# Sixteen tokens moved from dense products to gathered rows in the last stage of a one-core block

## The reference

```
act = gelu(einsum('ted,td->te', expert_u[e], t)) * gates
out = einsum('te,ted->td', act, expert_v[e])
```

## Time and profile before

| | |
|---|---|
| profiled execution, its own time | 4046.6 us |
| its span | 4045.0 us |
| clock granted to TensorE, mean | 0.996 |
| TensorE busy | 3982.8 us, 98% |
| TensorE's weight loads busy | 3441.5 us, 85%; one takes 188 ns |
| VectorE busy | 2477.6 us, 61% |
| ScalarE busy | 1227.1 us, 30% |
| GpSimd busy | 928.9 us, 23% |
| row steps (L1881) | 127 of 2346 ns, waits ahead of them 29.9 us |
| one-element gathers (L636) | 128 of 1535 ns |
| chain that ended last | TensorE 63%, VectorE 7%, DMA 4%, issue 3% |

### The profile page before, as it was taken

One profiled execution on the slowest core, in us unless ns is written; L12 is line 12 of the kernel. 1 busy time (PEld: TensorE's weight loads), 2 busy tenths in 40 slices (PEclk: granted clock), 3 DMA queues, 4 the chain that ended last, 5 costly groups with the idle time before them and its releaser, 6 DMA issues.

```text
span 4045.0 us, 53754 instructions
## 1 busy us (share of the span) xinstructions
PE 3982.8 (98%) x19149; PEld 3441.5 (85%) x19149; DVE 2477.6 (61%) x3455; ACT 1227.1 (30%) x1299; POOL 928.9 (23%) x670
## 2 busy tenths in 40 slices
PE   8999999999999999999999999999999999999998
PEld 5887777787788788888888888888899999999997
DVE  8565777469534654535676663222257787887885
ACT  4333222344223322222333332222222222222222
POOL 1100000332111345453000000000023444444432
PEclk9999999999999999999999999999999999999999
DMA  4543333652543454546777778666768888888883
GB/s 175 194 141 132 118 118 123 208 183 100 190 144 142 155 181 158 180 158 211 241 239 241 239 245 309 219 214 218 229 233 309 302 324 301 326 305 323 300 322 131
DMA packets 240049, 867.73 MB, mean 215 GB/s; under 512 B 22600, under 2 KB 61016, under 8 KB 172272
## 3 DMA queue, kind: packets, MB, share of 16 engines
q1 hardware_dynamic: 96720, 454.07, 30.7%
q10 hardware_dynamic: 94080, 204.49, 16.3%
q0 software_dynamic: 49184, 208.36, 14.8%
HBM read 768.25 MB, written 232.81 MB: 247 GB/s over the span
## 4 chain that ended last, share of the span: by engine, by line
PE 63%; DVE 7%; DMA 4%; issue 3%; ACT 2%; POOL 0%; DVEq 0%; SPq 0%; ACTq 0%
PE mm L1959 15%; PE mm L1960 15%; PE mm L1961 15%; DMA raw<-stream 3%; PE pv L1959 2%; PE pv L1961 2%; PE pv L1960 2%; DVE wlo L1127 2%; PE sc L1961 1%; PE sc L1960 1%; PE sc L1959 1%; DVE acc L1881 1%; ACT whi L684 1%; PE st L1961 1%; PE st L1960 1%
## 5 line engine op out<-in xcount | busy, mean ns | idle before, releaser
L1127 DVE TENSOR_TENSOR wlo<-raw,whi 128x2048 fp32r<-128x2048 f32 x329 | 756.2, 2299 | 762.0 <-ACT whi L684 757.4
L684 ACT ACTIVATE whi<-raw 128x2048 fp32r<-128x2048 f32 x378 | 723.7, 1915 | 492.6 <-issue 209.0
L1959 PE MATMUL mm<-t_hi,whi 128*128 128x512 f32 x2048 | 799.2, 390 | 4.3 <-DVE t_lo L1688 3.1
L1960 PE MATMUL mm<-t_lo,whi 128*128 128x512 f32 x2048 | 797.5, 389 | 0.0
L1961 PE MATMUL mm<-t_hi,wlo 128*128 128x512 f32 x2048 | 797.0, 389 | 0.0
L1959 PEld LDWEIGHTS mm<-t_hi,whi 128*128 128x128 f32 x2048 | 384.7, 188 | 86.1 <-DVE t_lo L1688 6.4
L1961 PEld LDWEIGHTS mm<-t_hi,wlo 128*128 128x128 f32 x2048 | 384.5, 188 | 80.4
L1960 PEld LDWEIGHTS mm<-t_lo,whi 128*128 128x128 f32 x2048 | 384.7, 188 | 77.5
L1959 PE MATMUL mm<-hn_hi,whi 128*128 128x512 f32 x960 | 377.4, 393 | 4.8 <-DVE wlo L1127 4.8
L1960 PE MATMUL mm<-hn_lo,whi 128*128 128x512 f32 x960 | 374.3, 390 | 0.0
L1961 PE MATMUL mm<-hn_hi,wlo 128*128 128x512 f32 x960 | 373.9, 389 | 0.0
(11 more groups left out here) (438 smaller groups left out, 7228.8 us busy)
## 6 DMA issues: line engine op xcount, KB each, us to landing
raw<-stream SPq DMA_DIRECT2D x380, 1024.0 KB
ev_d<-stream ACTq DMA_DIRECT2D x128, 1024.0 KB, 6.2
up_d<-sgl ACTq DMA_DIRECT2D x128, 256.0 KB, 2.1
g_d<-gst ACTq DMA_DIRECT2D x12, 2048.0 KB, 11.6
gg<-g_d SPq DMA_DIRECT2D x15, 1536.0 KB
gl<-up_d SPq DMA_DIRECT2D x120, 192.0 KB
spill<-stage ACTq DMA_DIRECT2D x44, 256.0 KB, 2.0
xm_d<-xms POOLq DMA_DIRECT2D x12, 512.0 KB, 5.5
```

The costliest lines, as they stand in the source:

```text
L684: act.activation(whi[:, k, :], raw[:, k, :], ACT.Copy).then_inc(hi_done, 1)
L1127: dve.tensor_tensor(wlo[:, k, :], raw[:, k, :], whi[:, k, :].bitcast(F32), ALU.subtract)\
L1959: pe.matmul(out, lh, rh, start=start, stop=False)
L1960: pe.matmul(out, lh, rl, start=False, stop=False)
```

## The change

Of the 384 dense tokens the last 16 (`TP` = 368 to 384) leave the products. `down` now multiplies 368 columns, and `add_down` adds 368. Gates, high and low halves are still made for 384.

Those 16 tokens are gathered with eight partitions a token (`LANES` = 8): partition p serves token p mod 16 and every eighth part of its 128 slots, so 16 more row steps (`LS`), each again 128 rows of 8 KB, into an accumulator of their own (`lane_acc`). In the last group at v = 3 sixteen products of `lane_acc` with a 128 x 16 matrix of ones and zeros (`lane_of`) sum the eight partitions of each token; `add_lanes` adds the result to `h2`.

The slots of the 16 tokens are brought into that layout through DRAM (three stores and one load on ScalarE's queue ahead of the one-hot stage), and VectorE computes the indices between two splits of the up stage.

The row steps are now 144 (`STEPS`): the first 16 for the lanes, 128 as before. They begin in group 0 at v = 2. All groups of VectorE are written out. GpSimd issues 16 one-element gathers for the lanes ahead of the first, and the batches of nine stand ahead of row 10 + 9b. `weights` stands directly ahead of the step that uses it first.

The tiles `gl` are now two with places of their own; some small tiles are added; some waits in the last group count the new product and its add.

```diff
+LT = 16
+TP = TD - LT
+LANES = P // LT
+LS = SLOTS // LANES
+STEPS = LS + SLOTS
...
-            activations(0)
-            for s in range(3, SLOTS):
-                if s % BATCH == 3:
-                    pool.wait_ge(ac_done, s // BATCH + 1)
-                    activations(s // BATCH + 1)
-                rows(s)
+            for s in range(LS):
+                activation_of(lane_el, lane_e, s)
+            for n in range(3, STEPS):
+                if n >= LS - 6 and (n - LS + 6) % BATCH == 0 and n - LS + 6 < SLOTS:
+                    b = (n - LS + 6) // BATCH
+                    pool.wait_ge(ac_done, b + 1)
+                    activations(b)
+                rows(n)
...
+                    act.wait_ge(slot_done, 2 * PH)
+                    for v in range(3):
+                        act.dma_start(lanes_d[:, :, v, :].rearrange("l t s -> t l s"), slot[P - LT:P, v, TB - 2, :, :]
+                                      .rearrange("p h k -> p (h k)").rearrange("p (l s) -> p l s", l=LANES))\
+                            .then_inc(lanes_moved, 16)
+            act.wait_ge(lanes_moved, 48)
+            act.dma_start(lanes[:], lanes_d.rearrange("l t v s -> (l t) v s")).then_inc(lanes_moved, 16)
...
-                    dve.tensor_tensor(h2[:, 4 * q + b, 0:TD], h2[:, 4 * q + b, 0:TD], vo2[q % 2][b][:, 0:TD],
+                    dve.tensor_tensor(h2[:, 4 * q + b, 0:TP], h2[:, 4 * q + b, 0:TP], vo2[q % 2][b][:, 0:TP],
                                       ALU.add).then_inc(v_free, 1)
+            def weigh(n):
+
+                dve.wait_ge(gv_in[n % 3], 16 * (n // 3) + 16)
+                to, w, s = (lane_acc, lane_ac, n) if n < LS else (acc, ac, n - LS)
+                if s == 0:
+                    dve.tensor_scalar(to[:], gv[n % 3][:], w[:, 0:1], None, ALU.mult).then_inc(acc_done, 1)
                 else:
+                    dve.wait_ge(acc_done, n)
+                    dve.scalar_tensor_tensor(to[:], gv[n % 3][:], w[:, s:s + 1], to[:], ALU.mult, ALU.add)\
                         .then_inc(acc_done, 1)
+            def lane_weights():
+
+                dve.wait_ge(el_in, 16 * LS)
+                dve.tensor_tensor(lane_ac[:], lane_el[:], lanes[:, 0, :], ALU.mult).then_inc(ac_done, 1)
+                dve.wait_ge(ac_done, 1)
+
+            def weights(b):
+
+                s0, s1 = BATCH * b, min(BATCH * (b + 1), SLOTS)
+                dve.wait_ge(el_in, 16 * (LS + s1))
+                dve.tensor_tensor(ac[:, s0:s1], el[:, s0:s1], gate3[:, s0:s1], ALU.mult).then_inc(ac_done, 1)
+                dve.wait_ge(ac_done, b + 2)
+
+            def gathered(steps):
+                for n in steps:
+                    if n == 0:
+                        lane_weights()
+                    if n >= LS and (n - LS) % BATCH == 0:
+                        weights((n - LS) // BATCH)
+                    weigh(n)
+
+            def down_group(g, steps):
+
+                dve.wait_ge(gn_in, 16 * g + 16)
                 for v in range(8):
                     down_lo(g, v)
...
                     gate((g + 1) % 2, v, 8 * g + 8 + v)
                     act_low(g % 2, v, 8 * g + 8 + v)
                     if v % 2 == 1:
                         add_down(g, v // 2)
+                    gathered(steps[v])
...
-            down_group(0, False)
-            down_group(1, True, peeled=True)
-            with dve.Fori(2, GROUPS_D - 1) as g:
-                down_group(g, True)
+            down_group(0, share((0, 0, 1, 1, 1, 1, 1, 1)))
+            for g in range(1, GROUPS_D - 1):
+                down_group(g, share((2, 1, 1, 1, 1 if g % 3 == 0 else 2, 1, 1, 1)))
...
-                        last = mm3(vo2[q % 2][b][:, 0:TD], *w(k, 512 * jj + P * b), actb[:, (g + 1) % 2, 0, 4 * h + jj, :],
-                                   actb[:, (g + 1) % 2, 1, 4 * h + jj, :], h == 0 and jj == 0, h == 1 and jj == 3)
+                        last = mm3(vo2[q % 2][b][:, 0:TP], *w(k, 512 * jj + P * b),
+                                   actb[:, (g + 1) % 2, 0, 4 * h + jj, 0:TP],
+                                   actb[:, (g + 1) % 2, 1, 4 * h + jj, 0:TP], h == 0 and jj == 0, h == 1 and jj == 3)
...
+                if v == 3:
+
+                    pe.wait_ge(acct_free, 1)
+                    for d in range(KC):
+                        last = pe.matmul(vo2[0][0][:, LT * d:LT * d + LT], lane_acc[:, P * d:P * d + P], lane_of[:],
+                                         start=True, stop=True)
+                    last.then_inc(acct_done, 1)
```

More of the change, by code:

```diff
@@ L220, in build @@
         acc = S("acc", [P, D], F32, 96)
+        lane_acc = S("lane_acc", [P, D], F32, 192)
+        lane_t = S("lane_t", [P, P], F32, 196)
+        lane_p = S("lane_p", [P, 3], F32, 196.5)
+        lane_f = S("lane_f", [P, 3, LS], F32, 196.625)
+        lanes = S("lanes", [P, 3, LS], F32, 205.25)
+        lane_v = S("lane_v", [P, LS], U32, 205.625)
+        lane_e = S("lane_e", [P, LS], U32, 205.75)
+        lane_el = S("lane_el", [P, LS], F32, 205.875)
+        lane_ac = S("lane_ac", [P, LS], F32, 206)
+        lane_of = S("lane_of", [P, LT], F32, 206.125)
         gv = [S(f"gv{i}", [P, D], F32, kb) for i, kb in enumerate((140, 148, 184))]
@@ L646, in _, with rows @@
-            for s in range(3):
-                rows(s)
+                    activation_of(el, idx_e, s)
+            def rows(n):
+                if n >= 3:
+                    pool.wait_ge(acc_done, n - 2)
+                index = lane_v[:, n:n + 1] if n < LS else idx_v[:, 0, n - LS:n - LS + 1]
+                pool.indirect_dma_start(gv[n % 3][:], None, ev_d, bass.IndirectOffsetOnAxis(ap=index, axis=0))\
+                    .then_inc(gv_in[n % 3], 16)
+            for n in range(3):
+                rows(n)
@@ L659, in _ @@
+            pool.wait_ge(acct_done, 5)
             pool.memset(sq_sum[:], 0.0).then_inc(qsum_done, 1)
@@ L1897, in down_group @@
+            def down_group(g, steps):
+                dve.wait_ge(gn_in, 16 * g + 16)
                 for v in range(8):
                     down_lo(g, v)
-                    if v == 0 and not slots:
-                        dve.wait_ge(gn_in, 16 * g + 16)
                     dve.wait_ge(upn_in[v % 2], 64 * g + 16 * (v // 2) + 16)
@@ L1919, in _, with share @@
             dve.wait_ge(h2_copied, 32)
-            down_group(0, False)
-            down_group(1, True, peeled=True)
-            with dve.Fori(2, GROUPS_D - 1) as g:
-                down_group(g, True)
+            at = [0]
+            def share(counts):
+                out = []
+                for c in counts:
+                    out.append(range(at[0], at[0] + c))
+                    at[0] += c
+                return out
+            down_group(0, share((0, 0, 1, 1, 1, 1, 1, 1)))
+            for g in range(1, GROUPS_D - 1):
+                down_group(g, share((2, 1, 1, 1, 1 if g % 3 == 0 else 2, 1, 1, 1)))
             def add_gathered():
@@ L1929, in add_gathered, with add_lanes @@
                                       vo2[0][b][:].rearrange("p (d t) -> p d t", t=P), ALU.add).then_inc(acct_free, 1)
-            last = BATCH * (GROUPS_D - 2)
+            def add_lanes():
+                dve.wait_ge(acct_done, 5)
+                dve.tensor_tensor(h2[:, :, TP:TD], h2[:, :, TP:TD],
+                                  vo2[0][0][:, 0:KC * LT].rearrange("p (d t) -> p d t", t=LT), ALU.add)\
+                    .then_inc(acct_free, 1)
             for v in range(8):
@@ L1935, in _ @@
                 if v == 0:
-                    weights(last, SLOTS - last, SLOTS)
-                    dve.wait_ge(ac_done, GROUPS_D - 1)
-                    for s in range(last, SLOTS):
-                        weigh(s, s % 3, s // 3 + 1)
+                    gathered(range(at[0], STEPS))
                 if v == 2:
                     add_gathered()
+                if v == 3:
+                    add_lanes()
                 if v % 2 == 1:
```

83 lines of the change are left out of this document (41 added, 42 removed).

## The result

The changed kernel took 4114.65 us (median of 4 runs, 4112.96 to 4117.77) against 4052.01 for the kernel before: ratio 1.0158, 95% interval 1.0144 to 1.0172. That is 63 us slower, where 4078 was forecast, outside the range of 4014 to 4108. The profiled execution took 4115.6 us, 69 more than that of before. TensorE's mean granted clock fell from 0.996 to 0.986.

A forecast was written before the change was run, and what follows sets the result against it. TensorE was taken to bound the kernel before, VectorE the changed one. Groups 2 to 14 +22, group 0 +8.8, group 1 -1.5 and the last +0.5 gave +30 us, so 4078, range 4014 to 4108.

The forecast's parts named there:

- gather batches: Groups 2 to 14: weights formed directly ahead of their step leave VectorE waiting at fourth rows, 62 us where 27.8 stood.
- Products: Down stage, TensorE: 6144 products lose 16 columns, 6.67 ns each, 41.0 us in all where TensorE stays the bound.
- rival D: TensorE's weight load is the bound, so fewer columns give nothing; 4084 us, chance 0.02.
- VectorE's own work: Groups 2 to 14: 721.6 us busy plus 70.3 of fixed wait, 60.9 a group against 64.0 of TensorE.
- Load leg: Groups 2 to 14: VectorE's waits for the high half of the weights and TensorE, 39 us, bounds 17 and 47.
- Group 0: First down group: VectorE stands 15 us for sixteen one-element gathers, so group 1 starts 8.8 us later.
- Group 1: Second down group, already written out: one more step fits at TensorE's pace, 66.5 becomes 65, -1.5 us.
- Last group: End of the down stage: units save 2.6 us, sixteen small fp32 products cost 3; net +0.5.
- Set-up: Up stage: 15 small VectorE operations and four small DMAs on ScalarE's queue cost nothing; possible stall taken as 0.
- B: Rival: the gather batches cost no more than before, 28 us instead of 62; 4043 us, chance 0.16.
- C: Rival: TensorE stays the bound, all DMA waits fit into 3.1 us a group; 4015 us, chance 0.19.
- E: Rival: fetching VectorE's some ten times longer program beside busy DMAs costs time; 4100 us, chance 0.05.

The follow-up runs named there:

- b_late: The kernel before with each batch's weights formed directly ahead of the group's first row step instead of at the group's head; 4094.77 us, ratio 1.0111.
- b_unroll: The kernel before with VectorE's groups 2 to 14 written out and nothing else; 4066.33 us (seven runs), ratio 1.0052.
- s_lump: a_spread with four more full-width VectorE operations in one place (ahead of the step of v = 5) in groups 2 to 14; 4139.2 us, ratio 1.0217.
- s_thin: a_spread with one more half-width VectorE operation ahead of the first step of every v in groups 2 to 14; 4109.57 us, ratio 1.0143.
- a_gn: The changed kernel with VectorE's wait for the gates moved behind the first split of a group; 4115.91 us, ratio 1.0164.
- a_spread: The changed kernel without batches: each one-element gather is issued behind a row gather, nine steps ahead of its use; 4034.76 us, ratio 0.9967.
- b_spread: b_unroll with each one-element gather issued behind a row gather instead of in batches, no tokens moved; 4042.83 us, ratio 0.9979.

## Why the prediction was wrong

The direction and the mechanism were right, the size was half: groups 2 to 14 lost 55 us where +22 was forecast. The step that failed is the price of the gather batches, 62 us for 86.2 measured; beside it the sum had no term for TensorE's clock.

*Products and rival D.* Products are 166.7 ns apart (3738.28 and 3738.45 above), as forecast. Rival D, the weight load as bound, is out.

*VectorE's own work.* Forecast 721.6 busy and 70.3 of fixed wait; measured 723.6 and 71.7. Load leg: forecast 39; measured 28.3 + 12.0 + 1.8 = 42.1. These terms held.

*The gather batches: the step that failed.* "The fourth row comes 24.0 us after the first step's start", and "Together 62 us". The positions were right: all thirteen batches stall at their fourth row, the longest (10.05, 9.7, 8.1) among those with a double step inside. But the time from first step to fourth row was 23.7 to 28.8 us, 25.8 in the mean of the thirteen. That is 13 x 1.8 = 23.4 us. The waits at the fourth rows came to 80.9, 18.9 more than forecast, as VectorE itself was a little later there; three at fifth rows (steps 56, 65 and 128), which the sum did not have, add 5.3. The 86.2 are 24.2 above the forecast and above its bound of 80, and most of the 33 us that the stretch lies above its forecast of 893.

The batch itself was mis-sized. It took 18.1 us in the mean (16.9 to 19.4) against 16.8 before (twelve batches, 16.1 to 17.4), and I had carried over the length of the earlier trace rows, 16.6; that is 1.5 of the 1.8 us. The two fences of one stall show why it is not a constant. The first gather starts inside the row step of 3701.44, which ends at 3703.79, and ends at 3704.63, 0.84 later. The next starts inside the split that ends at 3705.99 and ends at 3706.83, again 0.84 later. The one of 3707.13, which starts beside no long operation, takes 0.95. In groups 2 to 14 of the changed kernel 66 gathers were longer than 1.2 us. Each of them started inside a row step (37) or a split (29) and ended 0.8 us behind that instruction; the 51 short ones started beside neither. Placing the batch directly at a row step does not lengthen it by itself: in b_late it stands there too, and all twelve batches of groups 2 to 14 took 16.03 us. In its loop VectorE begins the step 0.39 us behind the start of the forming of the weights, and the first gather begins 0.04 later (the two lines under b_late): it took 0.95. In the written-out changed kernel the step begins 0.20 behind and the first gather 0.24 later, well inside it; in eleven of thirteen batches it took 2.95. These 2.0 us are nearly the whole way from 16.0 to 18.1. Written out at the old place, in b_unroll, ten of twelve batches took 17.7 to 18.7 us, with 51.6 us of waits. So it is the written-out code, at either place, that goes with the longer batches.

The Trainium skill (SBUF — State Buffer, "Who interferes with whom") says that whoever issues first gets the shared ports for a whole instruction and the other blocks fully. The trace agrees for gathers behind VectorE; the other way round it shows nothing of the kind: the 16 splits that started inside a gather of 0.95 us took 2.29 us, like the others. The section also holds, as inferred, that a `tensor_tensor` takes only the read side and does not hold up descriptor writing. 29 gathers outlasted a split, which is one; but a gather also reads its indices (`idx_e`) from SBUF, so no run here tells which of its parts was held up. I had weighed this rule only as a reason for shorter batches, since a stalled VectorE blocks nothing. The stall begins when most of the batch is over.

*The clock: a term left out.* The sum held no price for what follows a gap. The slower pace (22.3 us in groups 2 to 14, 18.2 of it in ten stretches at half speed, and 4.1 in group 0; before, 1.8 in all of these together) is the other side of the loss, and s_lump against s_thin shows that it is real time. It may not be added to the 24.2 above: the two are accounts of the same stretch, by VectorE and by TensorE. Part of VectorE's 42.1 of load leg is waiting for a TensorE at half speed; how much was not separated.

*Group 0.* Forecast: next split at 2988.5, fifth unit near 2991, group 1 at 3023. Measured: 2988.45, 2990.86, and 3025.7. The last 2.7 us are half-speed products behind the gap of 5.85 us. A wait for the gates had moved ahead of the first split, which the prediction did not read from the diff (7.70 us of VectorE, a second gap of TensorE); a_gn shows that it costs nothing, being ahead of the longer one. *Group 1*: 68.4, forecast 65; it had one gap of 2.7 us and 1.7 of slower pace where none were expected. *Last group*: +1.0, forecast +0.5. Sixteen fp32 products of 16 columns took 3.64 us, forecast 3 within 1.5 to 8:

```profile
4046.38 3.64 PE L2431 MATMUL pv<-lane_of,lane_acc 128*128 128x16 f32 x32
```

*Set-up.* The down stage began at 2946 instead of 2945: nothing, as said.

*The rivals.* B (28 us of stalls) and C (stalls fit) did not come in this schedule; a_spread comes near to C's world and lands at 4034.8 (C said 4015). E, code fetch, had nothing to show: in groups 2 to 14 no waits of VectorE put down to issue, and b_spread written out at TensorE's exact pace.

## What to carry to other kernels

A batch of small gathers on the queue that also feeds the main loop is a blackout. Its price is its length and the landing of the next row (25.8 us here) less what the buffers hold. Issue small gathers one by one between the large ones; here that turned +63 us into -15, and 9 of the 15 come without the change under study. Price a batch at the place, and in the code, where it will run: count the long VectorE operations that its members start under. And when a sum makes TensorE wait in one piece of several microseconds, add the products at half speed behind each gap; the same waiting in eight small pieces had almost none. A gain of the engine that is 99% busy is worth only the slack of the next one: 41 us of columns gave 13, 26 and nothing that can be told in three schedules.

## What the runs showed of the hardware

- A one-element indirect gather takes 0.95 us, or until 0.83 us behind the end of a 128 x 2048 row step or split inside which it starts (up to 2.99). Those that began at its very start did not lengthen: twelve in b_late began 0.04 us behind it and took 0.95. In a_spread, where each starts behind a row gather, the mean of all 128 was 1.24 us, in the changed kernel 1.73. Adds of 128 x 368 from PSUM did not lengthen any of the 12 that started under one.
- Half speed behind gaps: in the changed kernel's groups 2 to 14 there were eleven gaps of 3.3 to 9.0 us. Ten were followed by 8 to 18 products 0.31 us apart, one (of 3.4 us) was not, and neither was any of the shorter ones, the longest 2.9 us. A stretch cost 1.1 to 2.5 us. That is no limit to go by: in group 1 of the same run a gap of 2.7 us was followed by eleven such products. In the down stage of all fourteen traces every gap of 4 us and more (53 of them) was followed by at least eight; of the shorter ones some were (the shortest 2.2 us) and some were not (the longest 3.8).
- The same loop written out shortens VectorE's wait for ScalarE from 0.84 to 0.69 us a turn (86.9 to 71.7 us over 104 turns in b_unroll), and can still lose (b_unroll, 16 us).
